# Two low-part weight tiles made by an accumulating DMA within SBUF instead of VectorE subtractions

## What is computed

```python
h = rmsnorm(x, norm_pre_mix) * (1.0 + sc_m) + sh_m          # adaLN-modulated
proj = h @ w_in
(hq, hf, hi, hg, aq, ak, av, iq, ik, iw) = jnp.split(proj, split_points, axis=-1)
o_hg  = hgrn2_mixer(hq, hf, hi, hg, ...)    # 4 recurrent heads of 128 columns each
o_att = dsa_mixer(aq, ak, av, iq, ik, iw, ...)  # indexer scores, top-k, attention
y = concat([o_hg, o_att]) @ w_out           # then residual, SwiGLU feed-forward, residual
```

## Time and profile before

| | |
|---|---|
| median of 3 runs | 693.54 us (693.03 to 693.98) |
| profiled execution, its own time | 693.87 us |
| its span | 692.1 us |
| TensorE busy (matmul) | 680.6 us, 98% |
| VectorE busy | 555.7 us, 80% |
| ScalarE busy | 334.5 us, 48% |
| GpSimd busy | 135.1 us, 20% |
| granted TensorE clock | 1.0 throughout |

### The profile page before, as it was taken

The page is one execution under the profiler, slowest core; times in us unless marked ns, Lnnn a source line. Parts: engine busy times, 40 slices in busy tenths (PEclk is TensorE's granted clock), DMA queues, the critical chain, the costliest instruction groups (busy, mean ns, idle before and its releaser), DMA issues.

```text
span 692.1 us, 12998 instructions
## 1 busy us (share of the span) xinstructions
PE 680.6 (98%) x4640; PEld 567.9 (82%) x4640; DVE 555.7 (80%) x938; ACT 334.5 (48%) x569; POOL 135.1 (20%) x109
## 2 busy tenths in 40 slices
PE   7999999999999999999999999999999999999996
PEld 6566677777777878888788999999999998888885
DVE  3777999898898988988977799999999985344444
ACT  7357653545445344545753455555556551121123
POOL 4000000000000000000005567666766700000000
PEclk9999999999999999999999999999999999999999
DMA  9963222232224656568163255344433443322202
GB/s 274 357 207 95 61 63 62 75 107 61 62 62 119 217 183 217 179 230 254 31 183 91 71 145 149 115 130 130 131 110 114 122 131 126 109 92 91 61 10 112
DMA packets 97707, 88.92 MB, mean 128 GB/s; under 512 B 2735, under 2 KB 86787, under 8 KB 97670
## 3 DMA queue, kind: packets, MB, share of 16 engines
q1 hardware_dynamic: 97670, 88.44, 42.1%
HBM read 86.33 MB, written 2.10 MB: 128 GB/s over the span
## 4 chain that ended last, share of the span: by engine, by line
PE 62%; DVE 4%; issue 1%; ACT 0%; DVEq 0%; ACTq 0%
PE ps L2196 26%; PE ps L1690 17%; PE ps L1671 7%; PE ps L1708 6%; DVE rope L1104 1%; PE ps L2009 1%; DVE w_lo L1013 1%; PE ps L2029 1%; PE ps L2167 1%; PE ps L2174 1%; PE ps L1729 1%; PE ps L2169 1%; DVE act L1386 0%; DVE res L1391 0%; DVE act L1389 0%
## 5 line engine op out<-in xcount | busy, mean ns | idle before, releaser
L1671 PE MATMUL ps<-h_hl,w_hi 128*128 128x512 f32 x544 | 176.5, 405 | 0.0
L527 ACT ACTIVATE w_hi<-w_raw 128x1024 fp32r<-128x1024 f32 (+1 forms) x72 | 72.7, 1015 | 98.7 <-PE ps L1690 83.9
L1671 PEld LDWEIGHTS ps<-h_hl,w_hi 128*128 128x128 f32 x544 | 97.7, 188 | 24.6 <-issue 5.5
L1671 PE MATMUL ps<-h_hl,w_lo 128*128 128x512 f32 x272 | 106.6, 392 | 0.0
L2196 PE MATMUL ps<-h_hl,w_hi 128*128 128x256 f32 x576 | 104.5, 283 | 0.0
L2196 PEld LDWEIGHTS ps<-h_hl,w_hi 128*128 128x128 f32 x576 | 90.0, 192 | 0.2
L1013 DVE TENSOR_TENSOR w_lo<-w_raw,w_hi 128x1024 fp32r<-128x1024 f32 (+1 forms) x72 | 84.9, 1184 | 5.6 <-ACT w_hi L527 5.1
L1690 PE MATMUL ps<-w_hi,ht_hl 128*128 128x512 f32 x288 | 88.9, 389 | 0.0
L2196 PE MATMUL ps<-h_hl,w_lo 128*128 128x256 f32 x288 | 81.5, 283 | 0.0
L2196 PE MATMUL ps<-ht_hl,w_hi 128*128 128x256 f32 x432 | 78.5, 283 | 0.0
L2196 PEld LDWEIGHTS ps<-ht_hl,w_hi 128*128 128x128 f32 x432 | 67.4, 192 | 0.0
(11 more groups left out here) (310 smaller groups left out, 1260.2 us busy)
## 6 DMA issues: line engine op xcount, KB each, us to landing
w_raw<-in_w_ffn_in SPq DMA_DIRECT2D x44, 512.0 KB, 4.6
w_raw<-in_w_in SPq DMA_DIRECT2D x28, 512.0 KB, 4.0
w_raw<-in_w_ffn_out SPq DMA_DIRECT2D x22, 512.0 KB, 3.6
act<-in_w_ada SPq DMA_DIRECT2D x12, 512.0 KB, 8.4
adaw<-in_w_ada SPq DMA_DIRECT2D x6, 1024.0 KB, 5.2
act<-in_w_ada SPq DMA_DIRECT2D x6, 1024.0 KB, 5.2
res<-in_x SPq DMA_DIRECT2D x8, 512.0 KB, 5.6
w_raw<-in_w_out SPq DMA_DIRECT2D x8, 512.0 KB, 5.4
```

What stands on the lines that cost most here:

```text
L527: sc.activation(w_hi[slot][:, 0:n], w_raw[slot][:, 0:n], ACT.Copy).then_inc(hi_ok, 1)
L1671: last = mm(ps[bank][0:rows, :], a, b, start=(k == 0 and n == 0), stop=(k == KT - 1 and n == 2))
```

## The change

In head 0, for the third and fourth weight group only, ScalarE now writes the negated rounded weights into `w_lo` ahead of the high part, and GpSimd then issues a DMA that adds `w_raw` onto `w_lo` in SBUF, waits for its end and counts `lo_ok` up. VectorE's two subtractions are gone. VectorE waits for `lo_ok` 12 before the next low part that it makes itself, so that the count stays in order.

```diff
+        low_added = sem("low_added")
@@ gpsimd
             pool.memset(at_diag, 0.0).then_inc(at_zero, 1)
+            for j in (2, 3):
+                pool.wait_ge(hi_ok, G_HG + j + 1)
+                pool.dma_start(w_lo[j][:, :], w_raw[j][:, :], accum_op=ALU.add).then_inc(low_added, 16)
+                pool.wait_ge(low_added, 16 * (j - 1))
+                pool.sem_inc(lo_ok, 1)
             pool.wait_ge(att_out, ATT_HEADS)
@@ scalar
-            split_hi(2, U_HG[2], G_HG - 1)
-            split_hi(3, U_HG[3], G_HG)
+            for slot, free in ((2, G_HG - 1), (3, G_HG)):
+                sc.wait_ge(w_loaded[slot], U_HG[slot] * 16 + 16)
+                sc.wait_ge(group_done, free)
+                sc.activation(w_lo[slot][:, :], w_raw[slot][:, :], ACT.Copy, scale=-1.0)
+                sc.activation(w_hi[slot][:, :], w_raw[slot][:, :], ACT.Copy).then_inc(hi_ok, 1)
@@ vector
             rotate_iq(1, 2)
-            split_lo(G_HG + 2, 2)
             ve.wait_ge(lb_ok, 1)
...
             score_four(8)
-            split_lo(G_HG + 3, 3)
             rotate_iq(3, 4)
@@ vector, head 0
                 if isinstance(h, int) and h == 0:
+                    ve.wait_ge(lo_ok, G_HG + 4)
                     split_lo(G_HG + 4, 0)
```

## The result

The changed kernel takes 695.35 us (median of 14 runs, 694.39 to 698.05) against 693.52 us before (14 runs, 692.86 to 695.15): 0.25% slower, ratio 1.0025 with a 95% interval of 1.0016 to 1.0035. The forecast was 696.3 us in a range of 694.1 to 701.0. Its profiled execution took 696.71 us with a span of 695.0 us, so it is one of the slower ones.

A forecast was written before the change was run, and what follows sets the result against it. TensorE, busy 98% of the span, was taken to bound the kernel. ScalarE's 0.6 us plus the first DMA's stall of 2.15 us gave 2.75 us on 693.54, so 696.3 us, range 694.1 to 701.0.

The forecast's parts named there:

- TensorE passes a stall on whole and freed VectorE time is worth nothing: TensorE between 66 and 93 us: stalls reach the end whole; the 2.4 us of VectorE subtractions removed are worth 0.
- First term: ScalarE's two extra copies delay the fourth relu, VectorE's rotation and so TensorE's score 6: 0.6 us.
- GpSimd's issue at 73.2 us: The first DMA leaves at 73.2 us, behind two clearings in GpSimd's queue that wait for the sines.
- L: Time from the first DMA's issue to its landing: taken as 6.0 us, bounded by 3.6 and 8.6.
- Second term: TensorE stalls before step 16, waiting for slot 2's low part from the first DMA: L - 3.85 = 2.15 us.
- hidden rival: The first DMA lands in time (L at most 3.85 us), only ScalarE's 0.6 us remains: 694.1 us; chance 0.17.
- The second DMA hidden: Slot 3's DMA, counted at 85.4 us, is wanted by TensorE at 87.96: no stall, 2.5 us to spare.
- Faster: Rival: VectorE paces head 0 from 93 us on, its 2.4 us count: 691.7 us; chance 0.03.

The follow-up runs named there:

- ScalarE's copies alone: The kernel before with ScalarE's two negated copies added, VectorE's subtractions kept and overwriting them: 693.91 us against 693.45, ratio 1.0007.
- early DMAs: The changed kernel with GpSimd's two DMAs ahead of its two clearings: 694.47 us against 693.45 for the kernel before, ratio 1.0017.
- plain copy: The changed kernel with its two DMAs copying w_raw onto w_lo without the addition (low parts wrong): 694.51 us against 693.66 before, ratio 1.0016.
- the last kernel, with one small copy: The changed kernel with DMAs early, slot 3's ScalarE copies behind the sines, and one one-column VectorE copy: 693.70 us against 693.80 before, ratio 0.9998.
- three spread versions: The changed kernel with DMAs early and slot 3's ScalarE copies behind the sines; with none, one or two one-column VectorE copies: 693.65, 693.70, 693.87 us.
- the kernel without the subtractions: The changed kernel without negated copies or DMAs, so nothing replaces VectorE's two subtractions (low parts left out): 693.64 us against 693.45 before, ratio 1.0007.
- changed, again: The changed kernel, same program, run and profiled a second time: 695.28 us against 693.66 for the kernel before, ratio 1.0027.

## Why the prediction was right, point by point

- *TensorE passes a stall on whole and freed VectorE time is worth nothing.* Right for the stall: the 1.1 us between two profiles of the changed kernel came through whole. Freed time brought nothing, as forecast: every kernel without the subtractions is at best where it was. That it could cost something, the sum did not have (see *Missed*).
- *First term, ScalarE, 0.6 us.* Score 6 moved by 0.47 us, in the changed kernel and with ScalarE's copies alone, and 0.39 of it is left at the end of the way. The step that was too large is the 0.7 us that the fourth relu was to be late: it ends 2.97 us after the first score instead of 2.50, so 0.47. Closed up, ScalarE's instructions overlap by about 0.1 us each, and I had allowed one such overlap for the whole chain, where the three waits that went away make three. Score 6 started at 72.32 us, not 72.6 (first score 0.10 us earlier than before).
- *GpSimd's issue at 73.2 us*, set by the sines in its queue. 72.78 measured, early mostly by ScalarE's smaller delay. That this place is the cause is shown by the early DMAs, where the stall is gone.
- *L = 6.0 us, from the 1024 KB load plus 0.8.* 6.1 in the first profile, 5.0 in the second. *Second term 2.15 us*: step 16 moved by 2.01 and 0.92 us beyond score 6, and by 0.22 with the plain copy's 4.3 us. So the stall was L - 4.1, where the sum had L - 3.85: counted from the first score the DMA was issued 0.3 us earlier than forecast, and step 16 was wanted 0.1 us earlier. The median of the 14 runs, 1.83 us over before, fits the shorter landing: 1.83 - 0.47 - 0.45 (the two moves on VectorE, below) leaves 0.9 for this term, an L of 5.0. That is an estimate; the landing was seen in two runs only. So the central forecast was 0.9 us high in the median, and the term that was too large is this one, by 1.2 us: a single value of 6.0 stood for a landing that was 5.0 in one run and 6.1 in another. The reasoning for L was right in kind: the addition moves at about half the copy's rate. That the second operand read is the cause is argued from that rate, not shown.
- *The Trainium skill's two rules.* Plain copy in 3.2 us, by "DMA: Bandwidth & Descriptors", section "Anatomy of one DMA": measured 4.3 us for the plain copy, so this case's trace is 1.1 us over the rule for it. The additions that ran with no load beside them took 4.5 to 6.1 us, 1.3 to 2.9 us over the same figure, and the hidden rival, which this figure gave, did not come. VectorE blocking GpSimd's DMA, by "SBUF — State Buffer", its box on that: a landing 2.5 us longer than forecast did not show. Nor does the landing go with VectorE's busy time: a DMA that landed after 4.5 us had VectorE busy for 4.22 us of them, one of 5.3 us for 3.60 (both in the last kernel, with one small copy). A constant hold-up can't be told from these runs, since VectorE worked beside every one of the DMAs.
- *The second DMA hidden.* Right: no idle before step 24 in any kernel. It is slower than the first (6.5 and 6.7 us), beside the 512 KB load that the first count releases; where no load ran beside it, in the three spread versions, landings took 4.5 to 5.4 us.
- *Faster, 0.03.* Ruled out by the kernel without the subtractions: its ratio's interval begins at 0.9998, 0.1 us below before.
- *Missed:* 0.45 us in heads 1 and 2, from VectorE's instruction stream being one shorter. It stood nowhere in the sum: the prediction took VectorE's time there to be worth nothing either way. On the profiled execution, forecast and measurement are close (2.75 and 2.93 us) by luck, because this omission makes up for the excess of the two terms, 0.13 and 0.14; in the median it hides a part of the second term's excess.

The starts of the same matmuls, counted from the first score, close the sum. Each column is what the kernel has lost against the kernel before by then, in us (heads 1 and 2: the second block of the level matmuls, L1953 before, at 131.88 and 163.60 us there):

| kernel | score 6 | step 16 | head 1 | head 2 | end of the way |
|---|---|---|---|---|---|
| changed, first profile | 0.47 | 2.48 | 2.83 | 2.95 | 2.93 |
| changed, again | 0.45 | 1.37 | 1.75 | 1.83 | 1.83 |
| ScalarE's copies alone | 0.47 | 0.47 | 0.46 | 0.43 | 0.39 |
| subtractions out, nothing instead | 0.00 | 0.00 | 0.35 | 0.45 | 0.38 |
| DMAs early | 0.48 | 0.48 | 0.83 | 0.90 | 0.86 |
| plain copy instead of addition | 0.47 | 0.69 | 1.06 | 1.13 | 1.08 |

For head 1 the two rows are these, before and changed:

```profile
131.88 0.46 PE L1953 MATMUL ps<-act 128*32 128x32 f32 x32
```

```profile
134.61 0.46 PE L1961 MATMUL ps<-act 128*32 128x32 f32 x32 [0.35 <-DVE act L1352]
```

The idle in a row is up to 0.2 us less than the start's move (0.34 against 0.47 at score 6, nothing against 0.22 at the plain copy's step 16), as the matmul before it is drawn to a modelled end. So a stall is better read from starts than from idle brackets.

## What to carry to other kernels

Work taken from an engine that runs ahead buys nothing; ask first what the replacement waits behind. Here the DMA stood in GpSimd's queue behind two clearings, and it cost what its landing went beyond 4.1 us. Ahead of them the same DMA stalls nobody, and TensorE shows no wait for the clearings, which then end 6 us later. A transfer whose landing varies by a microsecond should be planned with that microsecond of slack, or the median hides what single runs lose.

## What the runs showed of the hardware that I had not expected

- An addition by DMA within SBUF moves 512 KB at 194 GB/s against 354 for a copy, starts 1.4 us after issue, and lands after 4.5 to 6.1 us with no load beside it and 6.2 to 7.2 us beside a 512 KB load (seven profiles).
- VectorE's gap of 0.48 us depends on one instruction more or less in a stream of 1561: it appears with 1560 and 1562, each time before the 320th record. The kernel before has a gap of 0.47 us too, in the last head (185.51 us, the 604th record), where it costs TensorE nothing; the kernels with 1561 all have it there, and the others don't. What the place stands for, the fetching of instructions or something else, the runs do not say.
- VectorE's four-column scaling took 0.78 us instead of 0.17 where GpSimd's second clearing ran (72.31 to 72.84) at the same time:

```profile
72.09 0.78 DVE L1275 TENSOR_SCALAR hg_par<-hg_par 128x4 f32<-128x4 f32 x1
```

  It ends at 72.87, with the clearing. In the four kernels with early DMAs, whose clearings run from 77 us on, it takes 0.16 to 0.17 us. This agrees with the Trainium skill, "SBUF — State Buffer", section "SBUF: two separate sides", which says that VectorE and GpSimd share one port pair, and that the instruction that starts first holds it to its end while the other waits. For VectorE and a clearing it says so of instructions in a two-port mode; that this scaling ran in one is not shown here.
